# Key tiles of x and meta tokens, ring places given back in halves, and a re-cut router tail in one hybrid decoder layer on one Trainium2 core

## The reference

```python
h = jnp.concatenate([meta, x], axis=1)                 # 16 + 256 rows
hn = rms_norm(h, attn_norm_w[l])
proj = hn @ w_in[l]                                    # 1024 -> 1024 conv, 256 q, 160 kv, 2048 gates
u_conv, q_lat, kv_lat, g_lin = jnp.split(proj, SPLITS, axis=-1)
y_conv = conformer_conv(u_conv, ...)                   # 31 taps, 512 channels
y_mla = mla(q_lat, kv_lat, pos, ...)                   # 8 heads, causal, the meta rows are keys of all
g = jax.nn.sigmoid(g_lin + gate_b[l]).reshape(B, L, 2, D_MODEL)
h = h + (g[:, :, 0] * y_conv + g[:, :, 1] * y_mla) @ w_out[l]
h = h + moe(rms_norm(h, ffn_norm_w[l]), router_w[l], router_b[l], w_gate_up[l], b_gate_up[l],
            w_down[l], b_down[l])                      # top 4 of 32 experts
return h[:, N_META:]

# moe, for each of 32 experts and its tokens:
gu = xb @ w_gate_up[e] + b_gate_up[e]                  # 1024 -> 2048
g, u = gu[:, :D_FF], gu[:, D_FF:]
act = (clip(u) + 1) * (min(g) * sigmoid(1.702 * g))
y += (act @ w_down[e] + b_down[e]) * gate              # 1024 -> 1024
```

## Time and profile before

| | us |
|---|---|
| median of 3 runs | 1123.82 (1122.59 to 1125.42) |
| the profiled execution | 1123.83 |
| its span, first to last instruction | 1121.7 |
| PE busy in it | 1058.2 (94%) |
| DVE, ACT, POOL busy | 279.2, 156.4, 30.7 |

### The profile page before, as it was taken

How to read it: one execution, slowest core, us unless ns; L and a number is a source line. 1 busy time by engine, 2 the same in 40 slices (tenths; PEclk the granted TensorE clock), 3 DMA queues, 4 the chain that set the end, 5 groups by cost and what they waited for, 6 DMA issues and landing times.

```text
span 1121.7 us, 14638 instructions
## 1 busy us (share of the span) xinstructions
PE 1058.2 (94%) x6199; PEld 481.8 (43%) x6199; DVE 279.2 (25%) x701; ACT 156.4 (14%) x326; POOL 30.7 (3%) x31
## 2 busy tenths in 40 slices
PE   8999999999999999989998989899989889889988
PEld 6778875643333333333333333333333333333332
DVE  1698852551111111111111111111111111001101
ACT  3453351410000000000000000000000000000101
POOL 1000062000000000000000000000000000000000
PEclk9999999999999999999999999999999999999999
DMA  9933298599999999999999999999999999999996
GB/s 291 331 102 110 90 315 351 227 436 429 430 433 430 431 434 430 430 431 432 432 432 432 432 431 432 432 430 430 434 431 431 432 434 432 431 431 427 431 422 253
DMA packets 42718, 432.86 MB, mean 386 GB/s; under 512 B 3875, under 2 KB 22638, under 8 KB 27998
## 3 DMA queue, kind: packets, MB, share of 16 engines
q1 hardware_dynamic: 42160, 432.21, 92.3%
q10 hardware_dynamic: 366, 0.15, 0.1%
q0 software_dynamic: 160, 0.04, 0.1%
HBM read 431.34 MB, written 1.05 MB: 385 GB/s over the span
## 4 chain that ended last, share of the span: by engine, by line
PE 60%; DMA 36%; ACT 1%; DVE 1%; issue 1%; ACTq 0%; DVEq 0%; SPq 0%
DMA arena<-in_w_gate_up 32%; PE psum L904 22%; PE psum L939 14%; PE psum L696 5%; PE psum L606 4%; DMA arena<-in_w_down 4%; PE psum L869 3%; PE psum L744 3%; PE psum L771 2%; PE psum L949 2%; PE psum L919 1%; PE psum L878 1%; PE psum L924 1%; ACT arena L1241 1%; PE psum L687 1%
## 5 line engine op out<-in xcount | busy, mean ns | idle before, releaser
L904 PE MATMUL psum<-arena 128*64 128x512 f32 x2048 | 464.4, 609 | 38.6 <-DMA arena<-in_w_gate_up 38.0
L904 PEld LDWEIGHTS psum<-arena 128*64 128x64 f32 x2048 | 148.6, 140 | 349.3 <-issue 291.7
L939 PE MATMUL psum<-arena 128*64 128x512 f32 x1024 | 227.4, 597 | 2.8 <-DMA arena<-in_w_down 2.8
L1549 DVE TENSOR_SCALAR arena<-psum 128x512 f32<-128x512 f32 x32 | 22.1, 691 | 728.4 <-PE psum L904 724.6
L939 PEld LDWEIGHTS psum<-arena 128*64 128x64 f32 x1024 | 71.7, 137 | 136.6 <-issue 130.9
L1228 ACT COPY arena<-psum 128x256 f32<-128x256 f32 x32 | 11.9, 372 | 556.6 <-PE psum L878 556.6
L949 PE MATMUL psum<-arena 64*128 64x512 f32 x256 | 63.6, 615 | 7.7 <-ACT arena L1241 7.7
L696 PE MATMUL psum<-arena 128*128 128x256 f32 x256 | 58.9, 380 | 0.3 <-ACT arena L1124 0.3
L1241 ACT COPY arena<-psum 128x512 f32<-128x512 f32 x32 | 18.7, 585 | 251.7 <-PE psum L939 251.7
L696 PEld LDWEIGHTS psum<-arena 128*128 128x128 f32 x256 | 47.7, 190 | 7.3 <-ACT arena L1124 0.5
L869 PE MATMUL psum<-arena 128*128 128x64 bf16 x1488 | 48.4, 193 | 2.2
(11 more groups left out here) (222 smaller groups left out, 553.5 us busy)
## 6 DMA issues: line engine op xcount, KB each, us to landing
arena<-in_w_gate_up SPq DMA_DIRECT2D x54, 4096.0 KB, 39.7
arena<-in_w_down SPq DMA_DIRECT2D x27, 4096.0 KB, 39.9
arena<-in_w_gate_up SPq DMA_DIRECT2D x20, 2048.0 KB, 15.1
arena<-in_w_down SPq DMA_DIRECT2D x9, 2048.0 KB, 13.9
arena<-in_w_in SPq DMA_DIRECT2D x9, 1024.0 KB, 6.2
arena<-in_w_in SPq DMA_DIRECT2D x8, 512.0 KB, 9.0
arena<-in_w_out SPq DMA_DIRECT2D x2, 2048.0 KB, 13.5
arena<-in_x SPq DMA_DIRECT2D x4, 512.0 KB, 14.0
```

What stands on the lines that cost most here:

```text
L904: last = mm(b[64 * half:64 * half + 64, :], xe[i][:, k, :], channels(slot_gu[slot][:, j, o:o + FF], half), start=(k == 0 and first), stop= ...
L939: last = mm(b[64 * c:64 * c + 64, :], aT[:, j, 64 * h:64 * h + 64], slot_dn[slot][:, j, c * 512:(c + 1) * 512], start=False, stop=(h == DC ...
L1549: ts(g_s, G, LIMIT, None, ALU.min).then_inc(S.g_ready, 1)
```

## The change

**Key tiles.** Tile 2 of the rows is now the 16 meta tokens and tiles 0 and 1 are 128 rows of x each, everywhere from `xpos` to the keys (`places(t)` says which columns of the 272 a tile has). The sum of squares of the meta rows moves from ACT to DVE, one x transfer falls away, `turned_in` of the tile (0, 0) stands before the scaling of tile 1, and "kv" starts with the first 144 columns. In the attention, the 16 meta columns of four steps are put side by side in `prob_meta` and transposed once for the four; ACT spreads them with two masked copies into `metaT`. The values of the meta rows are computed four times over (`ckvn4`) so that they stand at the right partitions.

**Halves.** Pieces 10 to 17 are loaded in two transfers of 1 MB (piece 10 in 0.5, 0.5 and 1 MB). PE counts `part_used` after the first half of a piece (for piece 0 after its first and second quarter), and the first transfer waits for that, the last one for `used` as before. Expert 3's gate-up is no longer loaded in pairs.

**Router tail.** The last part of 256 columns is two of 128. The first gather is written to two banks, and DVE takes the half in the first bank once PE has written that half (`xe_half`). `cnt` and half a residual product move behind expert 0's second piece, and the copy of the indices to float is gone.

```diff
-OUT_PARTS = [(0, 0, 512), (0, 512, 512), (1, 0, 512), (1, 512, 256), (1, 768, 256)]
+OUT_PARTS = [(0, 0, 512), (0, 512, 512), (1, 0, 512), (1, 512, 256), (1, 768, 128), (1, 896, 128)]
...
+    add(("xe", 0), 4, "xe_half", 1)
...
+EARLY = {RING10: [1, 2, None], **{RING10 + i: [2 + i, None] for i in range(1, 2 * GC)}}
+EARLY_WORDS = {k: [0, 1024, 2048, 4096] if k == RING10 else [0, 2048, 4096] for k in EARLY}
+ALONE = [gate_up_piece(3, 3)]
...
 def in_pairs(n, c):
 
-    return 2 < n < E - 2
+    return n > 2 and (n > 3 or c >= GC) and n < E - 2
...
-            sp.dma_start(xpos[0:META, 2, :], x[2 * P - META:SEQ, :]).then_inc(in_x[2], 16)
-            sp.dma_start(xpos[0:META, 0, :], a["meta_tokens"]).then_inc(in_x[0], 16)
-            sp.dma_start(xpos[META:P, 0, :], x[0:P - META, :]).then_inc(in_x[0], 16)
-            sp.dma_start(xpos[:, 1, :], x[P - META:2 * P - META, :]).then_inc(in_x[1], 16)
+            sp.dma_start(xpos[0:META, 2, :], a["meta_tokens"]).then_inc(in_x[2], 16)
+            for t in range(2):
+                sp.dma_start(xpos[:, t, :], x[t * P:(t + 1) * P, :]).then_inc(in_x[t], 16)
...
+            def load_early(k):
+
+                for i, value in enumerate(EARLY[k]):
+                    if value:
+                        sp.wait_ge(S.part_used, value)
+                    else:
+                        sp.wait_ge(S.used, k - RING10 + 1)
+                    load(*piece_number(k), k % RING10, EARLY_WORDS[k][i:i + 2], in_early[k] if value else None)
...
-                sp.wait_ge(S.h1_ready, 3 if k == 8 else 5)
+                sp.wait_ge(S.h1_ready, 3 if k == 8 else 6)
...
-            filled("ckv", project(fill("ckv")[:, 0:L], "kv", 0, P, 0, L))
+            b = fill("ckv")
+            pe.wait_ge(S.hn_ready, 2)
+            pe.wait_ge(S.hn_act, 1)
+            project(b[:, 0:META + P], "kv", 0, P, 0, META + P)
+            pe.wait_ge(S.hn_ready, 4)
+            filled("ckv", project(b[:, META + P:L], "kv", 0, P, META + P, P))
...
-                for i, tile in enumerate((0, 1) if t == 0 else (1, 0, 2)):
-                    n = min(P, span(t) - tile * P)
-                    last = nc.tensor.transpose(b[0:n, i * P:(i + 1) * P], prob[:, t, tile * P:tile * P + n], ident)
+                for tile in range(t + 1):
+                    last = nc.tensor.transpose(b[:, tile * P:(tile + 1) * P], prob[:, t, places(tile)], ident)
+                if s % 4 == 3:
+                    last = nc.tensor.transpose(b[:, 2 * P:3 * P], prob_meta[:, s // 4 % 2, :], ident)
...
-            b = fill("cnt")[:, 0:E]
-            mm(b, ones, maskt[:, 0, :], start=True, stop=False)
-            filled("cnt", mm(b, ones, maskt[:, 1, :], start=False, stop=True))
-            residual(1, 0, 256, 512)
-            gather_first(1).then_inc(S.gathered, 1)
             residual(1, 1, 0, 512)
+            filled(("xe", 0), gather_first(1, 0, GR))
+            gather_first(1, GR, KD).then_inc(S.gathered, 1)
...
             for c in range(GC):
+                if c == 2:
+                    residual(1, 0, 256, 512)
+                    b = fill("cnt")[:, 0:E]
+                    mm(b, ones, maskt[:, 0, :], start=True, stop=False)
+                    filled("cnt", mm(b, ones, maskt[:, 1, :], start=False, stop=True))
                 pe.wait_ge(*((S.xe_half, 1) if c == 0 else (S.xe_ready, 1)))
...
+                last = gate_up_part(first, c, gu_of(0)[c], first=True, last_stops=False,
+                                    parts=[(0, 0), (0, FF)] if c == 0 else [(0, FF)])
...
-                ts(prob[:, t, 0:span(t)], prob[:, t, 0:span(t)], prs[:, t:t + 1], None, ALU.mult
+                dve.wait_ge(S.zero_clear, 1)
+                at = 32 * (s % 4)
+                ts(prob_meta[:, s // 4 % 2, at:at + META], prob[:, t, 0:META], prs[:, t:t + 1], None, ALU.mult)
+                ts(prob[:, t, META:span(t)], prob[:, t, META:span(t)], prs[:, t:t + 1], None, ALU.mult
```

202 lines of the change are left out of this document (126 added, 76 removed).

## The result

The changed kernel takes 1130.58 us, the median of 10 runs (1127.0 to 1134.12); the kernel before, run beside it, 1123.19 (1122.15 to 1125.42). The ratio is 1.0064, with a 95% interval of 1.0050 to 1.0078. The prediction was 1117.8 us and faster; it is slower by 7.4 us, outside the range. The profiled execution took 1131.73 us, span 1129.9, against 1123.83 and 1121.7.

The account below looks back on a forecast made before the run. The weight stream was taken as the bound: its restart after the router, remaining bytes at 432 GB/s, and a fixed end. Gains of 3.25 (stream), 1.6 (head) and 1.2 (attention), 6.05 us off 1123.83, gave 1117.8 us; range 1115.0 to 1120.8.

Parts of the forecast that it names:

- Router tail, -1.4: From the last part of `w_out` to expert 0: moved product 0.89, dropped cast 0.2, narrower last part 0.3 us.
- Attention, -1.2: Twelve of sixteen attention steps have one transpose less, 0.11 us each; gain 1.2 us, between 0 and 1.4.
- Head, -1.6: Kernel's start: transposes end 0.5 us earlier and the projection no longer waits 1.09 us for DVE; range 0.5 to 1.9.
- Start of the stream, 4.0 us earlier: Weights after the router flow at 215.7 instead of 219.7 us, 1.4 from the tail and 2.6 from halving piece 10.
- Its losses, 0.2 and 0.55: Stream loses 0.2 us within piece 10 and 0.55 us at piece 14, leaving 3.25 of 4.0 us.
- The wait for `cnt` and expert 1: Later `cnt` holds up DVE's splits and the gather, so expert 1 starts at 233.2 us, 0.6 later than before.
- the stop at piece 14: Piece 14 waits for half of expert 1's first piece, so the stream stands still for 0.55 us.
- the slower rival: Queue runs dry between cut transfers of pieces 10 to 17: 11.5 us lost, 1129.3 us; chance 0.03.
- From there to the end, 0: After piece 14 later waits hold, the pairs with 0.5 us left, so the stream's 3.25 us gain reaches the total.
- the slower side: Outcome of a measurably slower kernel, above 1127.2 us; chance 0.03.
- The fixed end: After the last wait for weights, at 1070.03 us, PE work of fixed length follows.
- the frame of the argument: Time is the stream's restart after the router, plus remaining bytes at 432 GB/s, plus a fixed end.

Follow-up runs that it names:

- The kernel before with its loop moved: Kernel before, its three dummy products of 256 columns at PE's start made 14 of 40, so PE's loop stands 44 instructions further on: 1138.34 us (1.0107).
- the placed versions: Changed kernel, first turn written out, 76 or 88 always-holding waits ahead of the loop, three dummy products for five; four versions: 1123.05, 1122.65, 1122.16, 1121.23 us.

## Why the prediction was wrong, point by point

In the profiled pair the forecast was 6.05 us less, and it was 7.9 more. The terms:

- **Router tail, -1.4: right.** Expert 0 starts 1.9 us earlier (213.48 in the chain against 215.36), of which 0.4 was there when the tail began (174.47 against 174.86): 1.5.
- **Attention, -1.2: right.** From its start (68.31 against 67.18) to its end (145.27 against 145.29) it became 1.15 shorter.
- **Head, -1.6: wrong, +1.1 in this pair.** The scaled rows and squares did come earlier (DVE L1367 at 6.68), but I took for granted that PE would be free. Five dummy products stand ahead of the transposes, and their time was read from one profile as if it were fixed; it is 2.4 or 4.6 us. The identity came later besides, at 5.21 instead of 4.45. In the better case the first projection is 1.0 us earlier than before, nearer to the 1.6.
- **Start of the stream, 4.0 us earlier: right** (4.45 at SP's issue, 0.4 of it from ahead of the tail; 4.65 at 50 MB).
- **Its losses, 0.2 and 0.55: mis-sized.** From 50 to 100 MB it gave back 3.2 us instead of 0.75. The wait for `cnt` and expert 1 came as forecast (233.09 for the 233.2), so the stop at piece 14 was real; the slower rows of 4 and 8 KB were the part that I had set at nothing, on the strength of 403 GB/s at 44 to 56 us. In the earlier trace rows that is 7% under 432, and I should have charged it: 7% of the 16.8 MB of cut pieces is 2.7 us, an estimate from these two rows. The sign of the slower rival, GB/s visibly under 430, was seen (403 in slice 9), but not its mechanism: SP had the next piece queued, and the loss was nowhere near its 11.5 us.
- **From there to the end, 0: wrong, and most of the loss.** "A microsecond by which the stream starts earlier is one off the total, if the stream never stops again": stops of the stream were sought among the pieces and PE's work, and the sum had no term for the code of PE, which comes over the same transfer engines as the weights. Between 100 MB and the last wait for weights the changed kernel lost 7.1 us. It was not lost by PE's four stops: the first part of each transfer stayed 2.1 to 2.2 us ahead of the kernel before, and the last part, for which PE waits, fell from 0.4 us ahead to 5.7 behind while the code was loaded again. The kernel before with its loop moved went from 6.0 to 13.6 in the same way; the version with the first turn written out lost 0.1 between 100 and 430 MB. No rival had it, and the slower side had 0.03.
- **The fixed end: wrong by 2.6 us** (6.8 for 4.2 behind the last copy), also PE's code.

The four misses are 2.7, 2.45, 7.1 and 2.6 us. Tail, attention and the start of the stream were together 0.55 better (4.65 us at 50 MB, where 6.8 less the head's 2.7 is 4.1), and what lies outside the span 0.3 shorter. That makes 14.0 of the 13.95 us between forecast and result. The prediction had named the sign of it: if the last wait for weights ends otherwise than 6 us earlier, the frame of the argument is wrong.

With its code kept by writing out a turn and nothing else altered, the change gives nothing that can be measured (1124.09 us, 0.9997). With `cnt` late and fewer dummies as well, two of the placed versions (none cut, all cut) are 0.15 to 0.2% under the kernel before, at 1121.2 and 1122.2 us, the other two can't be told from it, and with one dummy product it is 1121.38 (0.9979, 0.9969 to 0.9989).

What stays open: why a packet of code sets its transfer engine back by 1.5 us; why these packets fall on eight of the 16 engines; what picks between the two cases of the head, and whether it is behind the spread of 4 to 7 us over the runs of one kernel.

## What to carry to other kernels

If an engine runs a long loop, look at the queue of kind instruction: packets that come at every turn, and an idle time called issue at the loop's start, mean that its code no longer stays loaded, and then a few instructions more or fewer anywhere ahead of it are worth more than the edit that one is weighing. The idle time is only what shows; here the price was paid where the code packets and a queued stream share transfer engines, and a transfer is done when its slowest part is. Whoever counts instructions should compare the count with the profile's number of products, since the place of a block's edge hangs on it. Compare the list of packets of two kernels before comparing anything else. And an earlier start of a stream is worth only what the next place to wait leaves of it: follow it to the first piece whose place another engine frees at a fixed time.

## What the runs showed of the hardware

- A loop of 1676 machine instructions on TensorE, 6.5 packets of 16 KB, ran its turns of some 140 us without a load between 348 and 937 us when it began 81 instructions behind a block's edge (0 to 92 in all runs of this kind); when it began 125 behind, every turn loaded about nine packets again and TensorE stopped 4.3 to 6.0 us, and when it began just ahead of an edge, 9.4 to 11.7 us.
- The stops of 5 us did not delay a queued stream of weights (the first parts of its transfers kept their time within 0.1 us); the packets of code did, in steps of 1.5 to 1.6 us for one of 16 parts, so that the spread between first and last part grew from 3.7 us to 11.5.
- With a jump near the end to code that isn't loaded the span ended 6.0 to 6.8 us behind the last copy, otherwise 4.2 to 5.1, in a kernel of 1120 us.
- The same five products of 256 columns (ten passes) at the start took 2.43, 3.0 or 4.6 us under the same granted clock of 1.00.
- While pieces cut into rows of 4 and 8 KB flowed, the weight stream ran at 382 GB/s with the transfer engines 96% busy, where uncut pieces gave 429 in the same window.
